# Delta rule: two steps' triangular inverses in one chain over two periods, key products in a bank of their own

## What is computed

```
decay = exp(where(incl, g[..., :, None] - g[..., None, :], -inf))
m = where(strict, einsum('bhncd,bhnsd->bhncs', k_beta, k) * decay, 0)
t_inv = triangular_solve(eye + m, eye)             # 64 x 64, per head and chunk
a_intra = where(incl, einsum('bhncd,bhnsd->bhncs', q, k) * decay, 0)
def step(state, inp):                              # one chunk after the other
    v_new = u_i - w_i @ state                      # u, w: t_inv times v, k
    o     = (q_i * exp(g_i)) @ state + a_i @ v_new
    state = state * exp(g_last) + k_dec^T @ v_new
```

## Time and profile before

| | us |
|---|---|
| median of 3 runs | 2008.03 (2002.91 to 2008.05) |
| profiled execution, its own time | 2007.89 |
| span of the profile | 2006.1 |
| TensorE busy in the span | 1937.5 (97%) |
| VectorE busy in the span | 1333.5 (66%) |
| the stage, from the first `pairs` to the end of its last work | about 340.6 to 661.8 |

### The profile page before, as it was taken

How to read it: one execution, slowest core, us unless ns; L and a number is a source line. 1 busy time by engine, 2 the same in 40 slices (tenths; PEclk the granted TensorE clock), 3 DMA queues, 4 the chain that set the end, 5 groups by cost and what they waited for, 6 DMA issues and landing times. The chain is left out here.

```text
span 2006.1 us, 38383 instructions
## 1 busy us (share of the span) xinstructions
PE 1937.5 (97%) x15923; PEld 1513.4 (75%) x15923; DVE 1333.5 (66%) x2184; ACT 819.2 (41%) x1536; POOL 390.0 (19%) x378
## 2 busy tenths in 40 slices
PE   7999999998988899999999999999999999999998
PEld 5888887466766687787676666787888888888887
DVE  5675323777766678564543566459988888877886
ACT  5122321544455345222222676445444444444342
POOL 3000001433444455011120361541000000000000
PEclk9999999999999899999999999999999999999999
DMA  6212333000000856821121310433322222269553
GB/s 220 59 43 71 100 89 133 24 4 3 4 4 3 296 180 240 307 85 49 59 74 63 143 48 3 168 91 128 115 82 77 90 73 90 85 226 350 194 194 137
DMA packets 192305, 220.97 MB, mean 110 GB/s; under 512 B 14240, under 2 KB 142212, under 8 KB 191492
## 3 DMA queue, kind: packets, MB, share of 16 engines
q1 hardware_dynamic: 182558, 190.59, 28.7%
q0 software_dynamic: 4640, 17.30, 2.2%
q10 hardware_dynamic: 4934, 10.61, 1.4%
HBM read 176.54 MB, written 41.94 MB: 109 GB/s over the span
## 5 line engine op out<-in xcount | busy, mean ns | idle before, releaser
L229 ACT ACTIVATE w_hi<-w_stage 128x1024 fp32r<-128x1024 f32 x88 | 93.1, 1058 | 307.0 <-PE acc L265 125.2
L263 PE MATMUL mix_acc<-mix_hi,w_hi 128*128 128x512 f32 x416 | 170.1, 409 | 0.0
L237 DVE TENSOR_TENSOR w_lo<-w_stage,w_hi 128x1024 fp32r<-128x1024 f32 x88 | 111.7, 1269 | 82.6 <-ACT w_hi L229 82.5
L265 PE MATMUL mix_acc<-mix_hi,w_lo 128*128 128x512 f32 x416 | 162.9, 391 | 0.0
L264 PE MATMUL mix_acc<-m_lo,w_hi 128*128 128x512 f32 x416 | 162.2, 390 | 0.0
L263 PE MATMUL acc<-h_hi,w_hi 128*128 128x512 f32 x400 | 158.9, 397 | 0.0
L265 PE MATMUL acc<-h_hi,w_lo 128*128 128x512 f32 x400 | 157.6, 394 | 0.0
L264 PE MATMUL acc<-h_lo,w_hi 128*128 128x512 f32 x400 | 156.3, 391 | 0.0
L809 DVE TENSOR_TENSOR raw<-acc,y_tok 128x1024 f32<-128x1024 f32 (+1 forms) x27 | 33.0, 1224 | 135.2 <-PE acc L265 129.6
L1868 PE MATMUL mix_acc<-mix_hi,w_hi 128*128 128x512 f32 x288 | 116.2, 403 | 5.8 <-DVE w_lo L237 3.2
L1869 PE MATMUL mix_acc<-m_lo,w_hi 128*128 128x512 f32 x288 | 113.1, 393 | 0.0
(11 more groups left out here) (532 smaller groups left out, 4972.2 us busy)
## 6 DMA issues: line engine op xcount, KB each, us to landing
w_stage<-in_w_in SPq DMA_DIRECT2D x48, 512.0 KB, 4.5
w_stage<-in_w_up SPq DMA_DIRECT2D x44, 512.0 KB, 4.7
w_stage<-in_w_out SPq DMA_DIRECT2D x32, 512.0 KB, 4.0
w_ada<-in_w_ada SPq DMA_DIRECT2D x32, 512.0 KB, 5.3
w_stage<-in_w_down SPq DMA_DIRECT2D x14, 1024.0 KB, 5.2
a_stage<-hidden_spill SPq DMA_DIRECT2D x12, 1024.0 KB, 6.6
hidden_spill<-hidden SPq DMA_DIRECT2D x22, 512.0 KB, 2.6
spill<-y_tok POOLq DMA_DIRECT2D x20, 512.0 KB, 5.1
```

The lines of the kernel that those rows point to most:

```text
L229: nc.scalar.activation(w_hi[:, slot], w_stage[:, slot], ACT.Copy).then_inc(w_hi_ready, 1)
L237: nc.vector.tensor_tensor(lo, w_stage[:, slot, 0:lo.shape[1]], hi.bitcast(F32), ALU.subtract).then_inc(w_lo_ready, 1)
L263: nc.tensor.matmul(acc[:, h, :], w_hi[:, slot, k, :], hi[:, k, tok], start=k == 0, stop=False)
L265: mm = nc.tensor.matmul(acc[:, h, :], w_lo[:, slot, k, :], hi[:, k, tok], start=False, stop=k == kts - 1)
```

## The change

- Two consecutive steps (`BATCH` 2, batch b is steps 2b and 2b+1) now go through one chain of groups. Each `corner_sum`, `inv_sum`, `corner_mask`, `inv_add` and `turn_inverse` handles 16 systems instead of 8. The ten groups stand in slots 0, 2, 4, 6, 8 of the even period and 0, 2, 4, 6, 7 of the odd one (`CHAIN_AT`).
- The products and decays are made two steps ahead: `pairs` and `decay_exp` of step s+2 in slot 1, `gram` and `scores_of` of step s+2 in slot 4. `gram` has a bank of its own, `gram_bank` (step 1 alone uses `tri`). `pair_keys` has 6 buffers in place of 4.
- `first_inverse` of the next batch stands in slot 8 of odd periods, ahead of that slot's window step on VectorE.
- The recurrence moves up: `v_sum`, `v_copy` to slot 3, `kv_sum` and the first `advance` to 5, `out_sum` and `out_add` to 6, the second `advance` to 7.
- `place_blocks` copies 8 blocks once in two periods. Fillers of the first period go from 7 to 14.

```
-        CHAIN = (("corner", 1, 3), ("corner", 0, 1), ("inverse", 1, 3), ("inverse", 0, 1), ("corner", 1, 4), ("corner", 0, 2),
-                 ("inverse", 1, 4), ("inverse", 0, 2), ("corner", 1, 5), ("inverse", 1, 5))
+        CHAIN = [(kind, lv) for lv in range(1, LEVELS) for kind in ("corner", "inverse")]
+        CHAIN_AT = dict(zip((0, 2, 4, 6, 8, 10, 12, 14, 16, 17), CHAIN))
...
                 def gram(n):
                     if n >= 2:
-                        pe.wait_ge(s_xu, INV_AT[n - 2, LEVELS - 1])
+                        pe.wait_ge(s_scores, scored(n - 1))
...
-                FIRST_FILL = {1: 1, 3: 3, 5: 1, 7: 2}
+                FIRST_FILL = {0: 3, 2: 3, 4: 3, 6: 3, 8: 2}
...
+                        if k == 1 and s + 2 < NCH:
+                            pairs(s + 2)
-                        if k == 4 and z >= 0:
+                        if k == 3 and z >= 0:
                             v_sum(z)
-                        if k == 5 and s + 1 < NCH:
-                            pairs(s + 1)
-                        if k == 7 and 0 <= z < NCH - 1:
+                        if k == 4 and s + 2 < NCH:
+                            gram(s + 2)
+                        if k == 5 and 0 <= z < NCH - 1:
                             kv_sum(z)
-                        if k == 8 and z >= 0:
+                        if k == 6 and z >= 0:
                             out_sum(z)
...
-                    if s + 1 < NCH:
-                        gram(s + 1)
...
                         if k == 7 and 0 <= z < NCH - 1:
-                            advance(z, 0)
-                        if k == 8 and 0 <= z < NCH - 1:
-                            out_add(z)
-                        if k == 9 and 0 <= z < NCH - 1:
                             advance(z, 1)
-                        if k == 9 and s + 1 < NCH:
-                            scores_of(s + 1)
-                            first_inverse(s + 1)
+                        if k == 8 and s % BATCH and s + 1 < NCH:
+                            first_inverse(s // BATCH + 1)
```

More of the change, by code:

```diff
@@ L871, in build @@
         state = sb("state", [P, 8, DN_DIM], F32, stS)
-        tri = [bank(f"tri{i}", where=stS) for i in range(2)]
+        tri, gram_bank = bank("tri", where=stS), bank("gram_bank", where=stS)
         value_bank = bank("value_bank", (P, DN_HEADS, DN_DIM), stS)
@@ L972, in build @@
[L972 to L980, removed]
-            if s + 1 < NCH:
-                masks, inverses = masks + 1, inverses + 2
-                MASK_AT[s + 1, 0], INV_AT[s + 1, 0] = masks, inverses
+            kind, lv = CHAIN_AT.get(s % BATCH * SLOTS + k, (None, 0))
@@ new lines, in chain_step, with scored @@
+            return (kind if s < NCH else None), s // BATCH, lv
+        BATCHES, PER_BATCH = NCH // BATCH, 2 * LEVELS - 1
+        CORNER_AT = {(b, lv): (LEVELS - 1) * b + lv for b in range(BATCHES) for lv in range(1, LEVELS)}
+        MASK_AT = {(b, lv): LEVELS * b + lv + 1 for b in range(BATCHES) for lv in range(LEVELS)}
+        SUM_AT = CORNER_AT
+        INV_AT = {(b, lv): PER_BATCH * b + min(2 * lv + 2, PER_BATCH) for b in range(BATCHES) for lv in range(LEVELS)}
+        def scored(n):
+            return n + 1 + n // BATCH
@@ L1523, in _ @@
                 decay_exp(0)
+                decay_exp(1)
                 split_hi(act, C1 + 1, (C1 + 1) % 2, loads(C1 + 1))
@@ L1577, in first_inverse @@
+                def first_inverse(b):
+                    n = BATCH * b % PAIR_BUFS
+                    keys = pair_keys[:, n:n + BATCH].rearrange("p j h i c -> p (j h) i c")[:, :, 1, :]
+                    first, start = corner_of(0).rearrange("p j h c -> p (j h) c"), inv[:, 1].rearrange("p j h c -> p (j h) c")
+                    dve.wait_ge(s_scores, blocks_copied(b) - 1)
                     for q in range(1, BLOCKS, 2):
@@ new lines, in first_inverse, with inv_add @@
+                    if b:
+                        dve.wait_ge(s_placed, PLACED0 + BATCH * BLOCKS * b)
+                    dve.wait_ge(s_ym, MASK_AT[b, 0])
+                    nc.vector.tensor_tensor(start, first, unit.unsqueeze(1).to_broadcast([P, SYSTEMS, BL]), ALU.add
+                                            ).then_inc(s_xu, 1)
+                    turn_inverse(b, 0)
+                def inv_add(b, lv):
+                    w = 1 << lv
+                    dve.wait_ge(s_xs, SUM_AT[b, lv])
+                    at = SYSTEMS * BL
@@ L1600, in inv_add @@
+                        turn_inverse(b, lv)
                         return
[L1601 to L1607 removed]
+                    if b:
+                        dve.wait_ge(s_vsum, BATCH * b)
@@ L1608, in inv_add @@
+                    for j in range(BATCH):
+                        first = at + j * DN_HEADS * BL
+                        for hf in range(2):
+                            kind = kind_of(j, hf)
+                            r = block_rows(2 * hf + 1 - kind)
+                            ins = nc.vector.tensor_copy(whole_inv[r, j, :, block_cols(kind)], tri[r, first:first + DN_HEADS * BL]
+                                                        .rearrange("p (h c) -> p h c", h=DN_HEADS))
                     ins.then_inc(s_xu, 1)
@@ L1752, in _ @@
                 scores_of(0)
+                scores_of(1)
                 dve.wait_ge(s_state0, 3)
```

222 lines of the change are left out of this document (109 added, 113 removed).

## The result

The changed kernel took 2019.55 us (median of 5 runs, 2018.44 to 2026.4) against 2008.03, a ratio of 1.0071 with a 95% interval from 1.005 to 1.0091. The forecast was 2008, no difference, with 2020 as the far end of its range. The ratios in this document compare all runs of two kernels, so they are not quite the two medians divided (here 1.0057).

What follows compares the result with a forecast made beforehand. TensorE was taken as the bound, busy 212.6 of 233 us. Gains (-29) and the new end of odd periods with its clock (+29) cancel, -0.3 in all: 2008 us, own range 2001 to 2015, 8 times in 10 from 1990 to 2020.

Steps and rivals of the forecast that it cites:

- The ends of odd periods: TensorE waits for VectorE's tail: 4.8 us in periods 5, 9, 13 and 2.3 in 3, 7, 11; 21.3 us in all.
- covered: Rival: window steps cover the end of odd periods, only some 5 of 29 us remain, 1984 us; chance 0.10.
- the clock holds: Rival: shorter waits at odd ends, only long ones bring a clock spell, of 1.2 us; 1998 us; chance 0.24.
- Groups and waits that go: Double groups of 0.61 us save 1.3 us in two periods; lost waits of kv_sum and gram some 1.2 us.
- Periods 4 to 13: Five pairs of periods at 36.8 or 34.3 us: 179.0 against 176.6 us, +2.4, before the clock term.
- Clock: Half-clock spells of 1.7 us after three long waits and half of the short ones at odd ends: +7.6 us.
- Periods 14, 15 and 16: No preparation left in 14 and 15, no group of an inverse in 16: -5.4 us and -3.6 us.
- Period 17: A chain as before: 0 change.
- The start: First group about 349.4 against 348.05; 7 more fillers and double groups in period 0: +3.5 us (+1.3 to +6).
- Periods 1 to 3: Fewer groups, v_sum and kv_sum sooner, the short wait in period 3 counted: -4.8 us.
- heavier slots that cover it: Period 1: its heavier slots were to cover the wait at the end of an odd period; no size of its own.
- slower: Rival: clock falls at all six odd ends, 3.3 us each, 20 us in place of 7.6; 2020 us; chance 0.24.

Runs made afterwards that it cites:

- e7_tail2: e1_order with VectorE's last steps ordered apart for each form of odd period (window's copy, second advance, first_inverse; or first_inverse ahead of the window's step): 1999.53 us.
- e4_fills: The changed kernel with 7 fillers in period 0 in place of 14: 2019.87 us, ratio 1.0048 to the kernel before.
- e8_fill24: e1_order with 24 fillers in place of 13 ahead of the first group of the first inverse: 2005.88 us, ratio 0.9991 to the kernel before.
- e5_act: e1_order with the eight block copies of batch 0 on ScalarE after slot 5 of period 1, not on GpSimd: 2001.33 us.
- e1_order: The changed kernel with state products ahead of the new batch's first group (subtract_state ahead of its mask), first_inverse behind the window's step: 2005.21 us.
- e10_lateq: e8_fill24 with the 2 MB load of the window's queries, and loads behind it, held back until first_inverse has ended: 2005.78 us.
- e12_split: e8_fill24 with the window's queries loaded in four pieces, each started after the one before has landed: 2002.69 us.

## Why the prediction was wrong, point by point

- **The ends of odd periods**, "the step on which all hangs": 4.8 and 2.3 us predicted, 4.04 to 4.30 and 2.14 to 2.52 measured, released by the lines named. Right, the long ones 0.5 to 0.8 us too dear. The rival "covered" falls, and so does "the clock holds": each long end was followed by a spell of more than 1.2 us lost.
- **Groups and waits that go.** 0.61 us predicted, 0.65 measured. `gram` and `kv_sum` without a wait: right.
- **Periods 4 to 13.** +8.8 us (185.4 - 176.6), predicted +2.4 and most of the +7.6 for the clock. TensorE's time without work grew by 8.6 (23.8 against 15.2), its busy time by 0.2: what the wide groups saved (7 us, as e7_tail2's busy time shows with the clock nearly whole), the clock took back. The sum had both terms, and was 1.2 us too high.
- **Clock.** After the three long ends 6.8 us each at 0.59, 0.66 and 0.60, after the first short one 0.75:

```profile
472.60:479.40 6.80, 6.80 (x117) 5.57 (x117) 1.42 (x5) 1.35 (x6) 0.00 (x0) 0.59 0.01 2
545.20:552.00 6.80, 6.80 (x134) 5.40 (x138) 1.42 (x5) 1.82 (x8) 0.00 (x0) 0.66 0.01 2
...
435.80:442.60 6.80, 6.80 (x186) 5.40 (x188) 3.58 (x12) 3.13 (x13) 0.00 (x0) 0.75 0.01 4
```

  That is 2.8, 2.3, 2.7 and 1.7 us lost in these four (6.8 times what is missing to 1.00), 9.5 in all, where 1.7 was counted for a spell. In all of periods 4 to 13 the mean of 0.93 is worth up to 13 us, against 7.6. So the term was mis-sized by 2 to 5 us, since the earlier trace rows were two microseconds of a spell and not its length. The Trainium skill, "TensorE: Matmul & The Clock Gate", Part 1, was weighed ahead: the clock follows the array's recent activity and drops to half when it idles. It points the right way here (each long end and two of three short ones were followed by half clock, the second, of 2.14 us, was not: its state products took 1.09 us), and the price of a long end lay between my 1.7 us and the rival's 3.3.
- **Periods 14, 15 and 16.** -5.4 and -3.6 predicted; -3.9 (34.85 to 30.94) and -3.5 (14.8 to 11.3) measured. The first gain is the smaller by half clock left over from the end of period 13 (the state products at 621.84 took 1.98 us in place of 1.09). Period 17, counted at 0, was 1.0 us shorter.
- **The start, the first step that failed.** "7 more fillers and double groups stand in period 0, partly at half clock: +3.5 (between +1.3 and +6)". The first group came 1.46 us later, as said (1.35), but period 0 grew by 6.5: 7.9 us in all, beyond the upper bound. The sum had left some 2 us for period 0. What the trace shows in it is 5.5 us more of TensorE's own time, at a mean clock of 0.65, and 1.0 us more of standing still, of which 0.9 are the two waits for instructions. So the term was mis-sized in TensorE's work at half clock, and it named nothing that feeds TensorE. That second limit stands close behind the first: three packets of `q8` begin in period 0 (near 354.8, 358.6 and 362.9 us), one in that of the kernel before, and the loads of the stage hold all 16 DMA engines as it begins. With fewer fillers (e4_fills) or at full clock (e8_fill24) TensorE stood for the packet instead (1.62, 3.6 us), and only with pauses between the loads did period 0 fall to 11.3. The 3 us over the 8.24 of the kernel before that are left even there come with 9.28 us of TensorE's work at a clock of 0.99.
- **Periods 1 to 3: -4.8, the second step that failed, and the larger.** Periods 2 and 3 alone gave -4.9 (37.7 against 42.6 us between their state products). Period 1, for which "heavier slots that cover it" was all that I wrote, gave +7.2: 5.3 us more of standing still and 1.9 more of TensorE's busy time, at a clock of 0.86. It is the one period in which VectorE, ScalarE and GpSimd all prepare the window, each for the next, and the batch put its eight copies on GpSimd, `first_inverse` on VectorE and the group on TensorE into that chain. e5_act takes 7.0 us of it back: 4.8 by the two orders of e1_order, 2.2 by another engine for the eight copies. The prediction moved `place_blocks` without a cost and never named GpSimd as a link.
- The errors add up: the start 4.4 over, periods 1 to 3 7.1 over (2.3 against -4.8), the rest together 0.6 under its sum. With the sum's -0.3 that is the 10.7 us of the stage; the median lies 11.5 us above 2008. The rival "slower" had the time, 2020, by luck: its clock term was nearer than mine, but periods 4 to 13, where it would act, came out 1.2 us below my sum, and the loss lay in periods 0 and 1, where it said nothing.

## What to carry to other kernels

When work is batched, price the periods at the edges as closely as the steady ones: there the engines that have room in the middle (GpSimd, VectorE) form a chain, and copies put on a free engine can be on the path. Put work that is ready in front of work that waits, on the waiting engine; changing the order on the producing engine alone moves the wait to another reader. And an idle row marked "issue" in the middle of one group is a reason to look at the DMA queues: more instructions in less time can meet a burst of loads.

## What the hardware showed

- TensorE's instructions come as packets of 16 KB on a DMA queue that shares the 16 engines with the loads. A packet began 1.0 to 1.1 us after the first group where the loads left pauses (e10_lateq, e12_split), and 3.9 us after it in e8_fill24, at the end of 4 MB of loads that kept the engines 98% busy from 341 to 352.3 us. There TensorE stood still for 3.6 us and went on 1.4 us after the packet had ended. Moving the burst moved the gap, pauses of the loads shrank it to under 1 us.
- Two groups of 32 x 32 products in one took 0.65 us in place of 2 x 0.37: 0.09 us saved.
- A spell of half clock moved rather than went: 0.99 in period 0 and 0.79 in period 1 in e12_split, 0.78 and 0.95 in e8_fill24, with the same fillers.
